# HGRN2 and state-space trunk step on one core: first norm from token rows, state-space output in place order, sampled decay behind the first scans, final rows turned early

## What is computed

```python
def _rmsnorm(x, gain):
    y = x * rsqrt(mean(x * x, axis=-1, keepdims=True) + EPS)
    return y * gain

x = x + 0.5 * swiglu(rmsnorm(x, ln_ffn1[i]), ffn1_w_in[i], ffn1_w_out[i])
h = rmsnorm(x, ln_mix[i])
x = x + mixer_i(h)           # HGRN2 for i = 0, S5 for i = 1
x = x + 0.5 * swiglu(rmsnorm(x, ln_ffn2[i]), ffn2_w_in[i], ffn2_w_out[i])

# S5: bu = B_bar u;  bu[0] += lam_bar * s0;  s_t = lam_bar s_(t-1) + bu_t
# y = Re(C s) + d * u;  z = gelu(y);  a, gate = split(z @ w_glu);  out = a * sigmoid(gate)
```

## Time and profile before

| | |
|---|---|
| three runs | 2374.03, 2377.11, 2382.39 us; median 2377.11 |
| profiled execution, its own time | 2376.15 us |
| its span | 2374.4 us |
| busy: PE, weight loads, DVE, ACT, POOL | 2304.1, 2273.2, 1216.3, 687.1, 2.8 us |
| mean granted clock of PE | 0.994 |

### The profile page before, as it was taken

The page is one execution under the profiler, slowest core; times in us unless marked ns, Lnnn a source line. Parts: engine busy times, 40 slices in busy tenths (PEclk is TensorE's granted clock), DMA queues, the critical chain, the costliest instruction groups (busy, mean ns, idle before and its releaser), DMA issues.

```text
span 2374.4 us, 42839 instructions
## 1 busy us (share of the span) xinstructions
PE 2304.1 (97%) x17594; PEld 2273.2 (96%) x17594; DVE 1216.3 (51%) x1714; ACT 687.1 (29%) x830; POOL 2.8 (0%) x15
## 2 busy tenths in 40 slices
PE   6999999999999979999999999999998999999998
PEld 6999999999999979999999999999987999999998
DVE  5756765456677665342344575234348443433433
ACT  3222222234434333221222322122353332211223
POOL 0000000000000000000000000000000000000000
PEclk9999999999999989999999999999999999999999
DMA  4233443242322114323422332232134423223222
GB/s 130 71 83 113 134 117 97 75 110 63 92 72 54 54 56 131 100 67 96 107 79 78 89 87 77 85 89 81 57 124 152 112 72 88 80 76 93 81 63 73
DMA packets 390944, 211.11 MB, mean 89 GB/s; under 512 B 22641, under 2 KB 385346, under 8 KB 390850
## 3 DMA queue, kind: packets, MB, share of 16 engines
q1 hardware_dynamic: 380114, 198.03, 29.9%
q10 hardware_dynamic: 10736, 11.77, 1.5%
HBM read 193.01 MB, written 20.94 MB: 90 GB/s over the span
## 4 chain that ended last, share of the span: by engine, by line
PE 88%; DVE 7%; issue 2%; ACT 2%; ACTq 0%; DVEq 0%
PE ps L1841 80%; PE ps L2020 2%; PE ps L1811 1%; DVE w_lo L1067 1%; DVE rstd L1088 1%; PE ps L2057 1%; PE ps L2073 1%; PE ps L2180 1%; DVE o_rs L1597 0%; PE ps L1931 0%; DVE t_a L1093 0%; PE ps L2049 0%; PE ps L2082 0%; ACT z_hi L993 0%; PE ps L2066 0%
## 5 line engine op out<-in xcount | busy, mean ns | idle before, releaser
L1841 PE MATMUL ps<-h_hi,w_hi 128*128 128x288 f32 x3328 | 727.0, 300 | 16.2 <-DVE t_a L1093 13.7
L1841 PE MATMUL ps<-h_hi,w_lo 128*128 128x288 f32 x3328 | 713.7, 296 | 0.0
L1841 PE MATMUL ps<-h_lo,w_hi 128*128 128x288 f32 x3328 | 713.6, 296 | 0.0
L1841 PEld LDWEIGHTS ps<-h_hi,w_hi 128*128 128x128 f32 x3328 | 536.9, 189 | 24.5 <-DVE t_a L1093 10.1
L1841 PEld LDWEIGHTS ps<-h_lo,w_hi 128*128 128x128 f32 x3328 | 537.4, 189 | 0.0
L1841 PEld LDWEIGHTS ps<-h_hi,w_lo 128*128 128x128 f32 x3328 | 537.1, 189 | 0.0
L1067 DVE TENSOR_TENSOR w_lo<-w_raw,w_hi 128x2048 fp32r<-128x2048 f32 (+3 forms) x184 | 369.8, 2010 | 146.1 <-ACT w_hi L673 144.1
L673 ACT ACTIVATE w_hi<-w_raw 128x2048 fp32r<-128x2048 f32 (+3 forms) x184 | 309.7, 1683 | 242.7 <-PE ps L1841 229.9
L1841 PE MATMUL ps<-g_hi,w_hi 128*128 128x288 f32 x1408 | 303.5, 296 | 0.0
L1841 PE MATMUL ps<-g_hi,w_lo 128*128 128x288 f32 x1408 | 302.7, 296 | 0.0
L1841 PE MATMUL ps<-g_lo,w_hi 128*128 128x288 f32 x1408 | 302.6, 296 | 0.0
(11 more groups left out here) (330 smaller groups left out, 1794.4 us busy)
## 6 DMA issues: line engine op xcount, KB each, us to landing
w_raw<-in_ffn_w_in_dram SPq DMA_DIRECT2D x176, 512.0 KB, 4.9
w_raw<-in_ffn_w_out_dram SPq DMA_DIRECT2D x64, 384.0 KB, 4.0
w_raw<-in_ffn_w_out_dram SPq DMA_DIRECT2D x64, 320.0 KB, 3.6
w_raw<-in_hgrn_w_in_dram SPq DMA_DIRECT2D x32, 512.0 KB, 5.4
w_raw<-in_s_w_glu_dram SPq DMA_DIRECT2D x16, 512.0 KB, 5.2
wc_d<-c_pow ACTq DMA_DIRECT2D x8, 512.0 KB, 3.6
wb_d<-wb_st ACTq DMA_DIRECT2D x8, 512.0 KB, 4.0
s_in<-in_state_hgrn_dram SPq DMA_DIRECT2D x8, 512.0 KB, 4.5
```

Of the source, the lines that this page charges most:

```text
L1841: ins = M.matmul(ps[:, 2 * s + h, 0:HALF], w[j][:, at:at + P], v[:, k, h * HALF:(h + 1) * HALF], start=k == 0 and n == 0, stop=k == ph.kt ...
```

## The change

- **Start.** The prompt rows come in two transfers, each half of the channels, with the sample between. Tile 0 is turned before the vectors are. The squares for the first norm are taken on the token rows themselves, 1024 columns with their sum in one instruction (`square_rows`), for five chunks; root and reciprocal are taken of one column per chunk; five ACT instructions write diagonals of the factors, and five products of ones with these spread them over the partitions, ahead of the last eighth of the first product. `take_rstd` copies them into `rstd`. The squares by channel, their sums, `sum_tokens(0)` and the long reciprocal go.
- **State-space layer.** A one-column square root, behind the last `lift` but one, has its function table loaded early. `sampled_decay` and the add that reads it follow the first tile's scans, in `rstd` and `sq` instead of the rotation's buffers. `z_hi` and `z_lo` are kept in place order, and the glu's add into x reads its result across places (`placed`). The last two tiles turn back into banks of their own; the order of the last glu products and of `last_states` changes.
- **End.** The square goes ahead of `y_n`. Seven eighths of three chunks are turned before the sums of squares.

```diff
+        def placed(ap):
+            return ap.rearrange("p (t n) -> p n t", t=LIFT)
...
+        def back_bank(ct):
+            return {NK - 2: 4, NK - 1: 6}.get(ct, 2)
...
         def turned_back(ct):
...
-            b = 4 if ct == NK - 1 else 2
-            return ps[:, b:b + 2, 0:HALF].rearrange("p h (t n) -> p h t n", n=BLOCKS)
+            return ps[:, back_bank(ct):back_bank(ct) + 2, 0:HALF]
...
         @block.scalar
         def _(act):
...
-            act.dma_start(x_rows[:, 0:CHUNKS, :], x_prompt[0].rearrange("(c p) d -> p c d", p=P)).then_inc(x_in, 16)
+            x_v, w = x_prompt[0].rearrange("(c p) d -> p c d", p=P), D_MODEL // 2
+            act.dma_start(x_rows[:, 0:CHUNKS, 0:w], x_v[:, :, 0:w]).then_inc(x_in, 16)
             act.dma_start(x_rows[0:SAMPLE, CHUNKS, :], x_sample.rearrange("b t d -> (b t) d")).then_inc(x_in, 16)
+            act.dma_start(x_rows[:, 0:CHUNKS, w:], x_v[:, :, w:]).then_inc(x_rest_in, 16)
             lam_rows = s5_a_re[0].rearrange("g p -> (g p)").rearrange("(s q) -> s q", q=P)
...
+                if r:
+                    act.wait_ge(ssq_done, m + (r - 1) * NK)
...
                 act.wait_ge(begun, 1)
+                if fill is not None:
+                    nc.scalar.activation(cols(h_hi, m), cols(x, m), ACT.Copy, scale=vec[:, bass.ds(m + gain, 1)])\
+                        .then_inc(h_hi_done, 1)
+                if r:
+                    nc.scalar.activation(sq[:], cols(x, m), ACT.Square).then_inc(sq_done, 1)
                 if r == len(NORMS) - 1:
                     nc.scalar.activation(cols(y_n, m), cols(x, m), ACT.Copy, scale=vec[:, bass.ds(m + gain, 1)])\
                         .then_inc(yn_done, 1)
-                elif fill is not None:
-                    nc.scalar.activation(cols(h_hi, m), cols(x, m), ACT.Copy, scale=vec[:, bass.ds(m + gain, 1)])\
-                        .then_inc(h_hi_done, 1)
-                nc.scalar.activation(sq[:], cols(x, m), ACT.Square).then_inc(sq_done, 1)
...
             act.wait_ge(vec_done, 1)
+            def square_rows(c):
+                n = P if c < CHUNKS else SAMPLE
+                act.wait_ge(x_rest_in, 16)
+                nc.scalar.activation(sq_rows[0:n, c, :], x_rows[0:n, c, :], ACT.Square,
+                                     accum_out=rows_rs[0:n, c:c + 1]).then_inc(rows_sq, 1)
             for m in range(NK):
                 if m == 2:
                     split(PH[0], 0, 0, None, None)
                 if m == 5:
                     split(PH[0], 1, 0, None, None)
                 norm_tile(0, m, (x_read, m + 1))
+                if 1 <= m <= CHUNKS + 1:
+                    square_rows(m - 1)
+                if m == CHUNKS + 1:
+                    act.wait_ge(rows_sq, CHUNKS + 1)
+                    nc.scalar.activation(rows_rs[:, 0:CHUNKS], rows_rs[:, 0:CHUNKS], ACT.Sqrt, scale=1.0 / D_MODEL,
+                                         bias=eps_t[:])
+                    nc.scalar.activation(rows_rs[0:SAMPLE, CHUNKS:], rows_rs[0:SAMPLE, CHUNKS:], ACT.Sqrt,
+                                         scale=1.0 / D_MODEL, bias=eps_t[0:SAMPLE]).then_inc(rows_root, 1)
+            act.wait_ge(rows_done, 1)
+            for c in range(CHUNKS + 1):
+                n = P if c < CHUNKS else SAMPLE
+                ins = nc.scalar.activation(rs_diag[0:n, c, 0:n], ident[0:n, 0:n], ACT.Copy, scale=rows_rs[0:n, c:c + 1])
+            ins.then_inc(diag_done, 1)
+            def take_rstd():
+                act.wait_ge(norm_full, 1)
+                nc.scalar.activation(rstd[:, 0:SEQ], ps[:, 4, :], ACT.Copy)
...
-                    if ph.name[1] == 0 and j == 0 and isinstance(i, int) and i == 0:
+                    if ph is PH[0] and j == 0 and isinstance(i, int) and i == 0:
+                        take_rstd()
+                    elif ph.name[1] == 0 and j == 0 and isinstance(i, int) and i == 0:
...
+                    if r == 4 and last and j == 0:
+                        nc.scalar.activation(table[:], eps_t[:], ACT.Sqrt)
...
+                    nc.scalar.activation(halves(z_hi[:, ct]), turned_back(ct), ACT.Copy).then_inc(z_hi_done, 1)
...
+                z_high(NK - 1)
                 act.wait_ge(f_full, 1)
-                nc.scalar.activation(fp_rows[:].rearrange("p r q -> p (r q)"), ps[0:ST, 6, 0:2 * P], ACT.Copy)\
+                nc.scalar.activation(fp_rows[:].rearrange("p r q -> p (r q)"), ps[0:ST, 4, 0:2 * P], ACT.Copy)\
                     .then_inc(f_done, 1)
-                z_high(NK - 1)
                 act.wait_ge(f_full, 2)
-                nc.scalar.activation(fs_rows[:].rearrange("p r h q -> p (r h q)"), ps[:, 7, :], ACT.Copy)\
+                nc.scalar.activation(fs_rows[:].rearrange("p r h q -> p (r h q)"), ps[:, 5, :], ACT.Copy)\
                     .then_inc(f_done, 1)
...
+                if r:
+                    dve.wait_ge(ssq_done, m + (r - 1) * NK)
+                    dve.wait_ge(sq_done, m + ((r - 1) * NK + 1))
+                    V.tensor_tensor(ssq[:], ssq[:], sq[:], ALU.add).then_inc(ssq_done, 1)
             def rest(ph, j, i):
...
+                    V.reciprocal(rstd[:], sq[:]).then_inc(rstd_done, 1)
+                    dve.wait_ge(rstd_done, r)
             def scaled(dst, s):
...
+                    dve.wait_ge(rows_root, 1)
+                    V.reciprocal(rows_rs[:, 0:CHUNKS], rows_rs[:, 0:CHUNKS])
+                    V.reciprocal(rows_rs[0:SAMPLE, CHUNKS:], rows_rs[0:SAMPLE, CHUNKS:]).then_inc(rows_done, 1)
...
+                crossed = sq[:, 0:2 * ST * DEC_BATCH].rearrange("p (r s b) -> p r s b", r=2, b=DEC_BATCH)
                 def sampled_decay():
-                    shape = [P, 2, ST, DEC_BATCH]
-                    t1, t2 = (t[:].rearrange("p r s n -> p (r s n)").rearrange("p (r s b) -> p r s b", r=2, b=DEC_BATCH)
-                              for t in rot_t)
-                    by = [lam8[:, q].unsqueeze(3).to_broadcast(shape) for q in range(2)]
+                    by = [lam8[:, q].unsqueeze(3).to_broadcast([P, 2, ST, DEC_BATCH]) for q in range(2)]
                     dve.wait_ge(sin_done, 1)
-                    link.begin(V.tensor_tensor(t1, s5_in[:], by[0], ALU.mult))
-                    link(V.tensor_tensor(t2[:, ::-1], s5_in[:], by[1], ALU.mult))
-                    link(V.tensor_tensor(sampled, t1, t2, ALU.add))
+                    link.begin(V.tensor_tensor(sampled, s5_in[:], by[0], ALU.mult))
+                    link(V.tensor_tensor(crossed[:, ::-1], s5_in[:], by[1], ALU.mult))
+                    link(V.tensor_tensor(sampled, sampled, crossed, ALU.add))
...
-                    V.tensor_tensor(places(z_lo[:, ct]), turned_back(ct), f32(places(z_hi[:, ct])), ALU.subtract)\
+                    V.tensor_tensor(halves(z_lo[:, ct]), turned_back(ct), f32(halves(z_hi[:, ct])), ALU.subtract)\
...
-                    V.tensor_tensor(s5_fs[:, :, :, tiles].rearrange("p r b s -> p r s b"), v[:, :, :, PROMPT_BLOCKS:],
-                                    sampled[:, :, tiles], ALU.add).then_inc(v_read, 1)
+                    def sampled_states():
+                        V.tensor_tensor(s5_fs[:, :, :, tiles].rearrange("p r b s -> p r s b"),
+                                        v[:, :, :, PROMPT_BLOCKS:], sampled[:, :, tiles], ALU.add).then_inc(v_read, 1)
+                    if ct:
+                        sampled_states()
...
                         z_rest(ct - 2)
+                    if not ct:
+                        sampled_decay()
+                        sampled_states()
...
                 scale_lifted(1)
                 for ct in range(NK):
...
-                    V.tensor_tensor(cols(x, m), cols(x, m), t_a[:], ALU.add).then_inc(gs_done, 1)
+                    x_m = cols(x, m).rearrange("p (n t) -> p n t", t=LIFT)
+                    V.tensor_tensor(x_m, x_m, placed(t_a[:]), ALU.add).then_inc(gs_done, 1)
...
                     pe.wait_ge(z_ready, NK)
+                    pe.wait_ge(f_done, 2)
...
             pe.wait_ge(consts, 3)
+            pe.wait_ge(x_in, 32)
+            tokens(0)
             pe.wait_ge(vec_in, 7 * 16)
             turn(ps[:, 0, 0:NVEC], vec_rows[0:NVEC, :], NVEC).then_inc(vec_full, 1)
-            pe.wait_ge(x_in, 32)
-            for m in range(NK - 2):
+            for m in range(1, NK - 2):
+                if m == NK // 2:
+                    pe.wait_ge(x_rest_in, 16)
                 tokens(m)
             pe.wait_ge(vec_done, 1)
...
                 if m == NK - 2:
-                    sum_tokens(0)
+                    pe.wait_ge(diag_done, 1)
+                    pe.wait_ge(x_read, NK - 1)
+                    for c in range(CHUNKS):
+                        M.matmul(ps[:, 4, c * P:(c + 1) * P], ones[:], rs_diag[:, c, :], start=True, stop=True)
+                    M.matmul(ps[:, 5, 0:SAMPLE], ones[0:SAMPLE, :], rs_diag[0:SAMPLE, CHUNKS, 0:SAMPLE],
+                             start=True, stop=True).then_inc(norm_full, 1)
...
-                    b = 4 if ct == NK - 1 else 2
```

(57 more changed lines are left out.)

39 lines of the change are left out of this document (20 added, 19 removed).

## The result

| | before | after |
|---|---|---|
| median of four runs | 2375.57 us | 2351.77 us |
| lowest to highest | 2372.80 to 2382.39 | 2349.72 to 2353.64 |
| ratio of the runs, 95% interval | | 0.9895, 0.9872 to 0.9919 |
| profiled execution: span, own time | 2374.4, 2376.15 | 2349.8, 2351.51 |
| granted clock of PE, mean | 0.994 | 0.995 |

The kernel is 1.05% faster. The rest came from something that the change does by the way: two small new tiles push others 64 bytes on in SBUF, and PE's products take less time each.

What follows compares the result with a forecast made beforehand. The prediction took TensorE, busy 2304 of 2374 us, as the bound, so only its waits could move time. Start 8.0, layer 4.7 and end 0.75 summed to 13.5 us, from 2377.11 to 2363.6, range 2356.5 to 2370.5.

Steps and rivals of the forecast that it cites:

- first product earlier: Start: w_lo begins about 17.9 with weights landed at 14.3, so PE's first product comes 2.7 us earlier.
- start in all: Start: first product 2.7, norm pause 3.8 and clock 1.5 sum to 8.0 us gained, from 5.9 to 9.5.
- PE's pause in the opening: State-space layer: PE's wait before the second block products grows from 2.47 to about 4.2 us.
- lower clock behind it: State-space layer: after the longer pause, 3 to 4 us of PE work at the lower clock, losing about 1.5 to 2.
- first state products later: State-space layer: late start 1.8 plus the clock loss put PE 3.5 us behind.
- third state products later: State-space layer: the lateness reaches DVE in round 2, then 2.0 us behind the kernel before.
- a round: State-space layer: contiguous z_hi and z_lo shorten each round from 7.63 to 6.85 to 6.9 us, with DVE binding.
- layer: State-space layer: last state products 1.3 us earlier plus a tail gain of 3.4, 4.7 us in all.
- Rival (a): State-space layer: the longer pause doesn't lower the clock; 1.7 us more gained, 2361.9, down to 2357; chance 0.27.
- (b): State-space layer: rounds give nothing because PE binds them; only 8.7 us gained, 2368.4, or 2370.5 with late weights; chance 0.14.
- (c): State-space layer: the clock falls in the 4.2 us pause and never recovers in the rounds; about 2402 us; chance 0.04.
- (d): Start: the diagonal is ready only after PE needs it, so a 3.8 us pause returns; 2368.9 us; chance 0.07.

Runs made afterwards that it cites:

- pace_addr: Kernel before with two unused 32-byte tiles behind eps_t, shifting vec and everything behind it by 64 bytes; 2367.76 us, ratio 0.9941.
- after_addr: Kernel after with table and rows_rs put in the unused end of vec, so all other tiles lie where they lay before; 2362.05 us, ratio 0.992.
- w64: Kernel before with the weight tiles (w_raw, w_hi, w_lo) 64 bytes further on and all else in place; 2365.23 us, ratio 0.9947.
- h64: Kernel after with h_hi and h_lo 64 bytes further on as well, weights where they are; 2352.52 us, ratio 0.9891.
- g64: Kernel before with g, o and z tiles 64 bytes further on, t_a and what follows 128, small tiles in place; 2363.55 us, ratio 0.9937.
- pace_q1: Kernel before with one more PE instruction at the start, a wait long satisfied, and no address changed; 2378.61 us, ratio 0.9995.
- decay_first: Kernel after with the decay of the sampled states and its add back ahead of the first scans; 2349.71 us, ratio 0.987.
- lo_off: Kernel after with the decay back first and 64 bytes more ahead of h_lo, w_raw, g_hi, g_lo and o_lo; 2343.49 us, ratio 0.9853.
- wlo_off: Kernel after with the decay back first, h, g, o and z in line with w_hi, w_lo alone 64 bytes off; 2350.09 us, ratio 0.988.
- rest64: Kernel before with small tiles behind eps_t and t_a onward 64 bytes off a multiple of 128, g_hi and g_lo at one; 2369.9 us, one run.
- b32: Kernel before with 32 bytes ahead of w_raw and 32 more ahead of g_hi; 2380.07 us, ratio 1.0007.
- mixed: Kernel after with 64 bytes more ahead of h_lo, w_raw, g_lo and o_lo; 2343.73 us over two runs, ratio 0.9845.

## Why the prediction was wrong

**The step that failed** is the first one: PE works on "one line of products that the change doesn't touch. So only what PE waits for can move the time". The instructions weren't touched; the addresses that they read were. Two lines of the diff, `table` and `rows_rs`, move g by 64 bytes, and that made 12 of the 24.6 us (12.6 by pace_addr, 12.1 by after_addr; 13.0 and 10.3 by medians). No case of the forecast held it, so the range couldn't either.

The other steps, against the kernel after and the pairs of equal places:

| step | forecast | measured |
|---|---|---|
| first product earlier | 2.7 (w_lo 17.9) | 1.9 here (w_lo 18.70; weights there at 15.35, not 14.3); 3.2 in after_addr (w_lo 17.38) |
| pause for the norm | 3.8 gone | gone |
| clock behind it | 1.00, 1.5 gained | 1.00 |
| start in all | 8.0 (5.9 to 9.5) | 5.5 here, 7.9 in after_addr, 10.2 from w64 to h64 |
| load of the root's table | 0.7 | root 3.12 us behind the norm's first sums, now 2.41: 0.7 |
| PE's pause in the opening | 4.2 | 4.60 |
| lower clock behind it | 3 to 4 us of work, 1.5 to 2 lost | 6.8 us, PE at work in 5.0 of them, 2.3 lost |
| first state products later | 3.5 | 3.7 |
| third state products later | 2.0 | 3.3 |
| a round | 6.85 to 6.9, from 7.63 | 6.86 (6.5 to 7.4), from 7.60 |
| last state products earlier | 1.3 | 0.4 |
| tail | 3.4 | 3.3 |
| layer | 4.7 | 3.7; 4.4 in after_addr; 2.3 from w64 to h64 |
| strided add into x | 0 | 0.52 us each, nothing on the path |
| end | 0.75 | 0.4; 0.6 in after_addr |
| edits in all | 13.5 | 12.2 to 13.2 by spans; 12.7 to 18.7 by medians |

(State products are PE's L2249, whose first one in the eight rounds stands 17.4, 23.2, 30.8, 37.6, 44.5, 51.9, 58.6 and 65.1 us behind the norm's sums, where it stood 13.7, 19.9, 27.5, 35.2, 42.8, 50.4, 58.0 and 65.5.)

(The 2.3 us lost are the lengths of the two groups of products that ran at the lower level: 2.81 and 3.06 us, where before has 1.61 and 1.97. The upper bound of the start, 9.5, doesn't follow from its terms either: 3.5 + 3.8 + 1.5 = 8.8.)

That the sum of the edits came near 13.5 is in part luck: in the kernel after, the start fell short of its term by 2.5 us and the layer by 1.0, and in the cleanest pair the start gave 2.2 more than its term and the layer 2.4 less.

**A second step failed, inside the layer.** Up to the first state products it held: 3.5 us late was the forecast, 3.7 came (1.9 of late start and 2.3 of clock, less 0.45 of a wait that is gone). Then the forecast sent this lateness "through the gelu, the turn back and z_hi" to DVE and had it shrink to 2.0; it came to 3.3 two rounds on. The path that ended last was another. SP issues the transfer of the fourth tile's wb only behind the loads that wait for the first state products (`y_full`), so all of their lateness goes into its issue, and PE's fourth block products wait for it. Before, then after (issue, and PE's start):

```profile
1780.90 0.43 SPq L581 DMA_DIRECT2D wb<-wb_d  x1
...
1786.77 1.61 PE L2156 MATMUL ps<-u_lift,wb 128*64 128x72 f32 x32 [0.52 <-DMA wb<-wb_d]
```

```profile
1769.04 0.43 SPq L596 DMA_DIRECT2D wb<-wb_d  x1
...
1774.87 1.61 PE L2225 MATMUL ps<-u_lift,wb 128*64 128x72 f32 x32 [0.85 <-issue]
```

Counted from the norm's sums the issue moved from 16.5 to 20.2 us and PE's start from 22.4 to 26.1, both by 3.7; PE starts 5.8 to 5.9 us behind the issue in either. The profile names no releaser for the 0.85 us, but these products wait for three things only, and the other two, u_lift and the read of the banks (s_fs), were done by 1771.2; DVE itself then stood idle for 2.7 us. So these 0.85 us are a wait for wb; without it the third state products would stand some 2.5 us late (an estimate, 3.3 less 0.85), nearer to the 2.0. A later round waited for wb again, for 0.6 us, and took 7.4 us. How much an earlier transfer would give back was not run.

Rival (a), that the clock holds, fell. Its evidence was a pause of 3.5 us that left the clock up, the one for z_lo near the layer's end. That pause is no sign either way: it is 3.48 us in before and in pace_addr, at the same place of the same instructions, and in pace_addr, as in g64 and pace_q1, the clock fell with it for 3.4 us (pace_addr, columns as in the earlier trace rows):

```profile
1824.00:1827.00 3.00, 2.28 (x9) 2.28 (x10) 2.86 (x2) 0.00 (x0) 0.00 (x0) 0.54 0.00 0
```

Pauses of 2.5 to 2.7 us in the opening went with a fall too in pace_addr, g64, pace_q1, decay_first, lo_off and wlo_off, but not in before, rest64, w64 or b32: the same code goes either way, and what decides stays open. Rivals (b), (c) and (d) fell too: the rounds gave 0.74 each in the mean, though two waits for wb stood among them; the clock came back; the diagonal was five microseconds early.

For the strides, by the Trainium skill (SBUF — State Buffer, "Door 1: The DMA port swizzle") reads and writes that go to a new 16-byte line each time pay; the trace agrees, with 0.57, 0.45 and 0.52 us for 576 columns, and steps of 32 and of 288 bytes have nearly the same price, though the instructions differ in how many of their operands have the step.

## What to carry to other kernels

When the engine that binds is 97% busy, ask of every change whether it moves a tile that this engine reads, and count matmuls in equal windows of both traces before the waits are read: 415 against 419 in 55 us shows it at once. A layout that holds streams and weights 64 bytes apart gave an even 132.2 ns, and makes two kernels comparable; compare kernels only with their tiles in the same places, or a change gets credit for its padding. When an engine comes late, look for transfers that are issued behind its work: they carry all of the lateness on, past engines that had room to spare. Here lo_off (2343.5 us) and mixed (2343.7) beat the kernel after (2351.8) with the same products and a few bytes of unused room; lo_off also has the decay back in its old place, which alone gave 2349.7 (decay_first), and they ran on other chips than the kernel after.
